# The bias table of a windowed attention: a scratch tensor with one row block per head instead of a 128-row pattern

## The reference

```
dist = BLOCK + r - c                       # r: query in its block, c: key in two blocks
bias = rel_bias[t5_bucket(dist)]           # 32 buckets, one column per head
logits = where(valid, logits + bias, -inf) # valid: 0 <= dist < 128 (and the key exists)
```

## Time and profile before

| | us |
|---|---|
| median of 3 runs | 922.59 (922.12 to 922.65) |
| the profiled execution | 922.59 |
| its span | 920.8 |
| TensorE matmul busy | 861.7 (94%) |
| VectorE busy | 647.3 (70%) |
| ScalarE busy | 487.0 (53%) |
| GpSimd busy | 6.2 (1%) |

### The profile page before, as it was taken

How to read it: one execution, slowest core, us unless ns; L and a number is a source line. 1 busy time by engine, 2 the same in 40 slices (tenths; PEclk the granted TensorE clock), 3 DMA queues, 4 the chain that set the end, 5 groups by cost and what they waited for, 6 DMA issues and landing times.

```text
span 920.8 us, 16502 instructions
## 1 busy us (share of the span) xinstructions
PE 861.7 (94%) x6722; PEld 830.8 (90%) x6722; DVE 647.3 (70%) x986; ACT 487.0 (53%) x680; POOL 6.2 (1%) x15
## 2 busy tenths in 40 slices
PE   5999998989889999999968999999996999999995
PEld 5999997979779999999967999898996899999995
DVE  4875687687678877787766696677777666655443
ACT  5652447444445666654445646788555544444450
POOL 0200000000000000000000000000000000000000
PEclk9999999979999999999977999999997899999998
DMA  9874656846052766659751485555664377765531
GB/s 330 245 214 135 194 173 204 214 155 228 26 162 90 220 185 181 186 180 325 260 180 46 139 264 170 141 181 150 200 201 137 103 241 230 228 207 171 181 107 46
DMA packets 148651, 166.41 MB, mean 181 GB/s; under 512 B 5488, under 2 KB 141680, under 8 KB 148576
## 3 DMA queue, kind: packets, MB, share of 16 engines
q1 hardware_dynamic: 146960, 162.82, 56.8%
q0 software_dynamic: 544, 1.49, 0.8%
q10 hardware_dynamic: 1072, 1.05, 0.3%
HBM read 164.10 MB, written 1.25 MB: 180 GB/s over the span
## 4 chain that ended last, share of the span: by engine, by line
PE 69%; DVE 9%; ACT 5%; issue 1%; DMA 1%; DVEq 0%; ACTq 0%
PE ps L166 47%; PE ps L412 22%; DVE X L145 2%; ACT FA L142 2%; DVE lor L145 2%; ACT hir L142 1%; DVE FA L145 1%; DMA raw<-in_w_out 1%; ACT L142 1%; DVE FA L149 1%; PE ps L169 1%; DVE INL L145 1%; DVE st L145 0%; DVE X L153 0%; ACT SQ L142 0%
## 5 line engine op out<-in xcount | busy, mean ns | idle before, releaser
L166 PE MATMUL ps<-INH,hir 128*128 128x256 f32 x1320 | 384.6, 291 | 15.9 <-DVE lor L145 10.9
L145 DVE TENSOR_TENSOR lor<-raw,hir 128x1024 fp32r<-128x1024 f32 (+1 forms) x268 | 310.3, 1173 | 125.0 <-ACT hir L142 111.1
L412 PE MATMUL ps<-INL,hir 128*128 128x256 f32 x1320 | 379.3, 287 | 1.0 <-DVE INL L145 0.6
L166 PE MATMUL ps<-INH,lor 128*128 128x256 f32 x1320 | 378.8, 287 | 0.0
L142 ACT ACTIVATE hir<-raw 128x1024 fp32r<-128x1024 f32 (+1 forms) x268 | 267.0, 1015 | 143.1 <-PE ps L412 130.6
L166 PEld LDWEIGHTS ps<-INH,hir 128*128 128x128 f32 x1320 | 258.7, 196 | 23.7 <-issue 12.0
L412 PEld LDWEIGHTS ps<-INL,hir 128*128 128x128 f32 x1320 | 258.5, 196 | 2.6 <-DVE INL L145 2.6
L166 PEld LDWEIGHTS ps<-INH,lor 128*128 128x128 f32 x1320 | 259.0, 196 | 1.1 <-issue 1.0
L166 PE MATMUL ps<-HIH,hir 128*128 128x256 f32 x608 | 173.7, 286 | 0.2 <-DVE lor L145 0.2
L166 PE MATMUL ps<-HIH,lor 128*128 128x256 f32 x608 | 172.0, 283 | 0.0
L412 PE MATMUL ps<-HIL,hir 128*128 128x256 f32 x608 | 172.0, 283 | 0.0
(11 more groups left out here) (128 smaller groups left out, 689.3 us busy)
## 6 DMA issues: line engine op xcount, KB each, us to landing
raw<-in_w_in SPq DMA_DIRECT2D x64, 512.0 KB, 4.5
raw<-in_mod_wT SPq DMA_DIRECT2D x48, 512.0 KB, 4.4
raw<-in_ffn_w_up SPq DMA_DIRECT2D x44, 512.0 KB, 4.6
raw<-in_w_ffn_in SPq DMA_DIRECT2D x44, 512.0 KB, 4.6
raw<-in_ffn_w_down SPq DMA_DIRECT2D x20, 512.0 KB, 4.9
raw<-in_w_ffn_out SPq DMA_DIRECT2D x20, 512.0 KB, 3.4
raw<-in_xa_wkv SPq DMA_DIRECT2D x16, 512.0 KB, 3.8
raw<-in_xa_wq SPq DMA_DIRECT2D x8, 512.0 KB, 5.8
```

Source lines behind the costliest of these rows:

```text
L145: return DV.do(lambda e: e.tensor_tensor(o, a, b, op), *w)
L166: return PE.do(lambda e: e.matmul(o, l, r, start=start, stop=stop, skip_group_check=True), *w, inc=inc)
L412: return PE.do(lambda e: e.matmul(o, *b, start=False, stop=stop, skip_group_check=True), inc=stop)
```

## The change

The `rel` array in the vector input has 8 columns instead of 128. The mask is loaded on 8 partitions. The product and the addition have 8 rows, one for each head. The scratch tensor is 8 x 128 x 384: each head's row is written 128 times, with a source that repeats it. The reads are 8 transfers, one for each head, over all 128 partitions, with a row step of 383.

```diff
-                    ("w_dt", 64), ("ib", 1), ("fb", 1), ("dtb", 1), ("alog", 1), ("rel", 128)):
+                    ("w_dt", 64), ("ib", 1), ("fb", 1), ("dtb", 1), ("alog", 1), ("rel", 8)):
...
-            t_ng = dma(neg, bass.AP(tensor=A["buckets"].tensor, offset=32 * 384, ap=[[0, 128], [1, 384]]), q=GP)
-            t = mm(b.ap[:, 0:384], V("rel", n=128, p=32), oh[0:32, :], t_bc, t_vec, *b.free, inc=True)
-            t = tt(gv, b.ap[:, 0:384], neg, ALU.add, t, t_ng)
+            t_ng = dma(neg[0:8, :], A["buckets"][32:40, :], q=GP)
+            gv = gv[0:8, :]
+            t = mm(b.ap[0:8, 0:384], V("rel", n=8, p=32), oh[0:32, :], t_bc, t_vec, *b.free, inc=True)
+            t = tt(gv, b.ap[0:8, 0:384], neg[0:8, :], ALU.add, t, t_ng)
             b.free = [t]
-            sv = nc.dram_tensor("toeplitz", [16, 8, 384], F32).ap()
-            t = dma(sv.rearrange("r h n -> (r h) n"), gv, t, q=GP)
+            scr = nc.dram_tensor("toeplitz", [8, 128, 384], F32)
+            sv = scr.ap()
+            t = dma(sv, gv.unsqueeze(1).to_broadcast([8, 128, 384]), t, q=GP)
             ts_ = []
 
-            for i in range(8):
-                src = bass.AP(tensor=sv.tensor, offset=127 - 16 * i, ap=[[8 * 384 - 1, 16], [384, 8], [1, 256]])
-                ts_.append(dma(BI[16 * i:16 * i + 16, :, :], src, t, q=GP))
+            for h in range(8):
+                src = bass.AP(tensor=sv.tensor, offset=h * 128 * 384 + 127, ap=[[383, 128], [1, 256]])
+                ts_.append(dma(BI[:, h, :], src, t, q=GP))
...
-    v[0:32, VEC["rel"]:VEC["rel"] + 128] = np.tile(np.asarray(a["rel_bias"]), (1, 16))
+    v[0:32, VEC["rel"]:VEC["rel"] + 8] = np.asarray(a["rel_bias"])
```

## The result

The changed kernel takes 938.59 us (936.93 to 939.18, 4 runs), beside 922.36 us for the kernel before in the same comparison: a ratio of 1.0173, with a 95% interval of 1.0154 to 1.0192. It is slower, as forecast, and by twice as much: 16.2 us, where the forecast was 8.3 over the profiled 922.6, and the time lies 0.6 us over the top of the range. Over 20 runs of the changed kernel the median is 938.1, over the range too, by 0.1.

What follows compares the result with a forecast made beforehand. TensorE was taken to bound the kernel (69% of the span), losing time only where made to wait. 922.6 - 0.7 (start) + 7.3 (late weight loads) + 1.7 (clock) = 930.9 us, range 921.2 to 938.

Steps and rivals of the forecast that it cites:

- Part 1, the start: Ahead of X and the first weights: smaller mask and vector inputs shorten TensorE's 2.30 us wait by 0.7, bounds 0 and 1.1.
- Part 2, matmul and addition: Matmul with 8 stationary columns and VectorE addition on 8 partitions: same 384 columns streamed, both costed at 0.
- Part 3, the write's rate: Scratch write of 1.57 MB from 8 partitions: 60 GB/s (bounds 45 and 200), 26.2 us alone.
- The 54 GB/s: Scratch write: rate estimated from the Trainium skill's 27.2 GB/s per port, two ports reached; total would be 2.5 us more.
- The eight engines: Scratch write: assumed to run on eight DMA engines, one per source row, 196 KB each at 7.5 GB/s.
- Part 4, the weight loads: Loads issued with or behind the scratch write: o's first tile lands at 61.2 against 53.9, TensorE waits 7.3 us.
- Engines share by bytes: DMA queues beside the scratch write: each 512 KB tile passes with equal bytes of the write, 32 KB per engine, 5.7 us.
- six tiles: Loads issued with or behind the scratch write, v0's second half to o's first, landing from 32.7 to 61.2.
- The clock after the wait: TensorE after its 7.3 us wait: lowered granted clock costs 1.7 us more.
- Part 5, the table's lateness: Mask addition at line 666: table ready at 72.2, allowed until 72.4 with TensorE already late, so cost 0.
- The cheap write: Rival: write ends by 40, table stands at 51, nothing waits, 921.9 us; chance 0.28.
- The late table with unhurt loads: Rival: slow write doesn't delay weight loads, only line 666 waits, middle 4 us, 925.9 us; chance 0.14.

Runs made afterwards that it cites:

- e_near8: Inputs, matmul and addition of the kernel before, with the changed kernel's scratch write (from partitions 0 to 7) and reads; 937.25 us, ratio 1.018.
- e_ports: As e_near8, with the eight source rows taken from partitions 0, 9, ..., 63 instead of 0 to 7; 921.03 us, ratio 1.0004.
- e_packed: The changed kernel, with v's tiles and o's first two loaded from an array holding 4 KB in a row for each partition; 929.45 us, ratio 1.0087.
- e_actq: The changed kernel, with the scratch write issued by ScalarE instead of GpSimd; 935.38 us, ratio 1.0154.
- e_src16: Inputs of the kernel before; the same 1.57 MB scratch written from partitions 0 to 15, each row 64 times; 923.38 us, ratio 1.0021.

## Why the prediction was right and wrong

**Part 1, the start: right in its kind, a little too small.** 0.7 was taken, bounds 0 and 1.1; the matmuls shifted by 1.26 to 1.37, over the upper bound. In the changed kernel it brought nothing, as e_near8 shows: the wait for the write's landing ate it. The sum took it off all the same.

**Part 2, matmul and addition: right.** The addition takes 0.54 us on 8 partitions.

**Part 3, the write's rate: right in its cause, 60 GB/s against 48 measured.** The reason given, that the rate goes with the partitions reached, was refined by e_ports: not their number but their place. The 54 GB/s that the prediction worked out from the Trainium skill's port figure was nearer. The eight engines, an assumption, fit the 46.9% of sixteen.

**Part 4, the weight loads: the step that failed.** "Engines share by bytes" was read off the window 7 to 8. There three queues moved about equal bytes, but with 18 packets beside 58 and 57, and the trace doesn't say on how many engines each of them had work: the window could not tell the two rules apart. The changed kernel's 52 packets beside 49, e_ports' 71 beside 71 and e_packed show alternation by packets, once it has set in. A tile of 32 packets of 1 KB on an engine then passes beside 32 packets of 4.6 KB, not beside 32 KB of the write. So not six tiles passed with the write, one each 5.7 us. The first one, v's, landed at 58.8 instead of 32.7, and the three issued behind the write all landed with its end (58.8 to 61.8). ScalarE wanted v's tile at 39.4; the prediction gave no time by which it was needed. TensorE waited 16.8 us for it, where 7.3 for o's were forecast. The forecast named the right engine, the right releaser and the right mechanism (a slow packet holds the others up), but the wrong tile and half the price.

**How much of the miss is the rate.** The prediction's own sum with the measured 48 GB/s, 6.0 on an engine, has 5.5 + 1.3 us a tile, o's at 67.6 and 922.6 - 0.7 + 13.7 + 1.7 = 937.3, inside the range. So a nearer rate alone would have given nearly the right time, for the wrong reason. And the write landed at 59.5, where 61 was forecast, by luck: it is slower than assumed, but the loads hardly held it up (their packets take 2.8% of the engines beside its 46.9).

**The clock after the wait: undersized, and partly given back.** 1.7 was taken; 2.7 were lost up to o's tile. Later 1.9 came back where the kernel before had run at 0.64 and 0.51; this was not foreseen.

**Part 5, the table's lateness: right.** It cost nothing; the reads ended before line 666 was reached. The reads were faster than before, 5.7 us against 7.3.

**The rivals.** The cheap write would have been about right with source partitions 9 apart: e_ports is that case but for the inputs, ratio 1.0004 against the 0.9992 forecast for it. The late table with unhurt loads is refuted by the 19.41 us wait for a raw tile. The range's top, 938, was built from a slower write (50 GB/s) under the same wrong sharing and a room of 2 us; the 938.59 lie over it.

## What to carry to other kernels

A broadcast from a few neighbouring partitions to memory is no cheap transfer, even where nobody waits for it: it runs at those partitions' rate (48 GB/s here for eight), keeps its DMA engines busy all that time, and lets other queues' loads through one packet at a time or, for 15 us in e_actq and e_src16, hardly at all. Before giving a hidden transfer a price of nothing, ask which loads are issued behind it and how many packets a tile has on one engine. Spread the source (8 rows from partitions 9 apart: 13 us instead of 33.5), or write fewer copies.

## What was not expected of the hardware

- The same eight rows took 33.5 us from partitions 0 to 7 and 13.0 from 0, 9, ..., 63; the time of the whole kernel went from 937.25 to 921.03 by the step of one slice.
- Beside a write with half of the engines' time the other queue got about one packet for each of its own (52 and 49, 71 and 71, 156 and 157). But from 36 to 38 in e_actq it got none beside 63, with a tile under way. Beside the same bytes on sixteen engines it got 4 for 112, and 13 for 111 with packets of 4 KB. The cause is open.
- With the small inputs TensorE's idle ahead of the matmul of 14.60 was 0.67 to 1.44 us in five traces, and the granted clock from 14 to 22 stayed at 1.00 in all of them. With the larger inputs the same idle was 1.59 to 3.05 us in seven traces, and the clock was 0.57 to 0.79 in five. The other two, with 1.59 us and, in the kernel before, 2.30 us, kept 1.00.
- Small reads of the table spread over 128 partitions landed in 2.4 us in a quiet stretch (e_ports), those of 16 partitions in 7.3.
